# The gate table's one-hot tensors, weighed on GpSimd instead of on ScalarE and VectorE

## The reference, cut to what matters

```python
sc = einsum("thpc,hpnc->thpn", q, sub_keys)        # two halves p, 128 keys each
top_s, top_i = top_k(sc, 16)                       # per token, head and half
best_s, best_pos = top_k(cand_s, 16)               # of the 256 sums of pairs
idx  = i * 128 + j                                 # i, j: the keys of the two halves
gate = softmax(best_s)
hid  = gelu(x . u[idx]) * gate
out  = sum over the 128 picks of hid * v[idx]
```

## Time and profile before

| | us |
|---|---|
| Median of 3 runs | 2608.36 (2605.65 to 2610.68) |
| The profiled execution's own time | 2611.84 |
| Its span, first to last instruction | 2610.0 |
| TensorE busy | 2421.7 (93%) |
| VectorE busy | 1398.1 (54%) |
| ScalarE busy | 738.3 (28%) |
| GpSimd busy | 396.8 (15%) |
| Line 1053, VectorE one-hots, 96 instructions | 113.0 busy, mean 1218 ns |
| Line 1093, ScalarE weighing, 288 instructions | 89.4 busy, mean 389 ns |
| Line 757 in this phase, GpSimd fetches, 65 instructions | 103.2 busy, mean 1587 ns |

### The profile page before, as it was taken

One profiled execution on the slowest core, in us unless ns is written; L12 is line 12 of the kernel. 1 busy time (PEld: TensorE's weight loads), 2 busy tenths in 40 slices (PEclk: granted clock), 3 DMA queues, 4 the chain that ended last, 5 costly groups with the idle time before them and its releaser, 6 DMA issues. The chain is left out here.

```text
span 2610.0 us, 26901 instructions
## 1 busy us (share of the span) xinstructions
PE 2421.7 (93%) x10289; PEld 1765.2 (68%) x10289; DVE 1398.1 (54%) x2491; ACT 738.3 (28%) x1319; POOL 396.8 (15%) x305
## 2 busy tenths in 40 slices
PE   7999899799999988988989999999995999987989
PEld 4467666687555555656668888889994898875444
DVE  1235423336987967465367777766676523346021
ACT  1134412222110134435233333333333322221010
POOL 1100000000233324132121111123330000023000
PEclk9999999999999999999989999999997899986999
DMA  4220032212777767787899999977772222120210
GB/s 179 92 81 17 9 129 98 96 65 77 242 249 251 244 205 240 232 262 220 263 359 309 314 312 309 311 259 277 274 258 101 101 97 97 49 105 3 78 65 32
DMA packets 181808, 454.45 MB, mean 174 GB/s; under 512 B 15536, under 2 KB 105904, under 8 KB 174896
## 3 DMA queue, kind: packets, MB, share of 16 engines
q1 hardware_dynamic: 144816, 318.49, 36.2%
q0 software_dynamic: 36864, 134.23, 14.9%
HBM read 406.33 MB, written 46.33 MB: 173 GB/s over the span
## 5 line engine op out<-in xcount | busy, mean ns | idle before, releaser
L722 PE MATMUL bank<-XT,ur 128*128 128x384 f32 x1552 | 523.1, 494 | 30.9 <-DMA ur<-in_u 30.9
L722 PEld LDWEIGHTS bank<-XT,ur 128*128 128x128 f32 x1552 | 293.5, 193 | 234.4 <-DMA ur<-in_u 43.6
L1224 PE MATMUL bank<-Vh,Hh 128*128 128x512 f32 x768 | 300.3, 391 | 12.7 <-DVE Vl L1273 12.4
L1226 PE MATMUL bank<-Vh,Hl 128*128 128x512 f32 x768 | 300.4, 391 | 0.0
L1225 PE MATMUL bank<-Vl,Hh 128*128 128x512 f32 x768 | 300.3, 391 | 0.0
L757 POOL DMA_INDIRECT ring_c<-in_v,gidx x128 | 148.0, 1156 | 501.6 <-DVE x_res L769 390.2
L1273 DVE TENSOR_TENSOR Vl<-Vr,Vh 128x1024 fp32r<-128x1024 f32 x128 | 156.8, 1225 | 116.6 <-ACT Vh L1247 116.5
L1247 ACT ACTIVATE Vh<-Vr 128x1024 fp32r<-128x1024 f32 x128 | 135.5, 1059 | 250.3 <-PE bank L1226 222.2
L1224 PEld LDWEIGHTS bank<-Vh,Hh 128*128 128x128 f32 x768 | 144.8, 189 | 43.4 <-issue 13.0
L1053 DVE TENSOR_TENSOR hot<-tab_sb,ijg 128x1024 f32<-128x1024 f32 x96 | 113.0, 1218 | 105.5 <-PE bank L1079 98.9
L731 ACT ACTIVATE ar<-bank 128x384 f32<-128x384 f32 x97 | 47.5, 490 | 428.0 <-PE bank L722 428.0
(11 more groups left out here) (305 smaller groups left out, 4173.9 us busy)
## 6 DMA issues: line engine op xcount, KB each, us to landing
ur<-in_u SPq DMA_DIRECT2D x128, 512.0 KB, 3.5
Vr<-in_v SPq DMA_DIRECT2D x128, 512.0 KB, 5.2
W<-in_w_stream SPq DMA_DIRECT2D x27, 2048.0 KB, 7.7
gates<-stage SPq DMA_DIRECT2D x48, 512.0 KB, 6.3
Gr<-gates SPq DMA_DIRECT2D x128, 192.0 KB
early<-ar SPq DMA_DIRECT2D x97, 192.0 KB
A<-early SPq DMA_DIRECT2D x97, 192.0 KB
w_raw<-in_w_mixer SPq DMA_DIRECT2D x14, 1024.0 KB, 4.9
```

What stands on the lines that cost most here:

```text
L722: mm = pe.matmul(c.bank[bank + r][:, 0:DN], c.ur[:, r, k * P:(k + 1) * P], c.XT[:, k, 0:DN], start=k == 0, stop=k == KT - 1)
L1224: pe.matmul(ps, Hh[r][:, tok], Vh[r][:, cut], start=n == 0, stop=False)
L1226: mm = pe.matmul(ps, Hl[r][:, tok], Vh[r][:, cut], start=False, stop=n == PK - 1)
```

## The change: what it does

The one-hots are made in the other order, `hot[0]` first. GpSimd weighs all 8 tokens of `hot[0]` with one product of 128 x 1024 by a broadcast operand; ScalarE's six instructions and VectorE's one per slice are gone, with their semaphores. TensorE waits for both one-hots and for GpSimd's product. GpSimd's fetches are no longer issued ahead: each iteration waits for the first one-hot of slice j, makes the product, and then issues one fetch, or seven after the last slice of a tile.

```diff
--- before.py
+++ after.py
@@ -1029,7 +1029,6 @@
     Q = 4
     S = 2 * Q
     NSL = P // S
-    ON_ACT = 6
     EB = 4
     CUTS = 16
     PER = E_LOOP + E_GAP
@@ -1037,8 +1036,7 @@
         hot = [[ctx.enter_context(nc.sbuf_tensor(f"hot{half}{i}", [P, S, P], F32)) for i in range(2)] for half in range(2)]
         stage = ctx.enter_context(nc.sbuf_tensor("stage", [P, PK, P], F32))
         gat.buffers(ctx, "ring_b")
-        hot_made, weighed_a, weighed_d, built, copied, stored = signals(
-            nc, ctx, "hot_made weighed_a weighed_d built copied stored")
+        hot_made, weighed, built, copied, stored = signals(nc, ctx, "hot_made weighed built copied stored")
         block = ctx.enter_context(nc.Block())
         dest = t["gates"].rearrange("i j t -> j i t")
 
@@ -1049,11 +1047,8 @@
                 r, tok = j % 2, j * S
                 if j >= 2:
                     dve.wait_ge(built, 2 * (j - 1))
-                for half in (1, 0):
+                for half in (0, 1):
                     dve.tensor_tensor(hot[half][r][:], mid(c.iota, S), bc(ijg[:, half, tok:tok + S], P), ALU.is_equal).then_inc(hot_made, 1)
-                dve.wait_ge(hot_made, 2 * j + 2)
-                part = hot[0][r][:, ON_ACT:]
-                dve.tensor_tensor(part, part, bc(ijg[:, 2, tok + ON_ACT:tok + S], P), ALU.mult).then_inc(weighed_d, 1)
                 gat.dot(dve, s)
                 s += 1
                 if j % NSL == NSL - 1:
@@ -1070,8 +1065,8 @@
                 e = E_GATES + tt * PER
                 for s in range(NSL):
                     j, r = tt * NSL + s, s % 2
-                    pe.wait_ge(weighed_a, j + 1)
-                    pe.wait_ge(weighed_d, j + 1)
+                    pe.wait_ge(hot_made, 2 * j + 2)
+                    pe.wait_ge(weighed, j + 1)
                     for q in range(2):
                         if 2 * j + q >= 4:
                             pe.wait_ge(copied, 2 * j + q - 3)
@@ -1085,23 +1080,12 @@
 
         @block.scalar
         def _(act):
-            def weigh(j):
-
-                act.wait_ge(hot_made, 2 * j + 2)
-                for k in range(ON_ACT):
-                    one = hot[0][j % 2][:, k]
-                    last = act.activation(one, one, ACT.Copy, scale=ijg[:, 2, j * S + k:j * S + k + 1])
-                last.then_inc(weighed_a, 1)
-
             for tt in range(DT):
                 e = E_GATES + tt * PER
-                weigh(tt * NSL)
                 if tt >= 1:
                     act.wait_ge(stored, 16 * CUTS * tt)
                 for s in range(NSL):
                     j = tt * NSL + s
-                    if s + 1 < NSL:
-                        weigh(j + 1)
                     for q in range(2):
                         act.wait_ge(built, 2 * j + q + 1)
                         o = stage[:, :, (2 * s + q) * Q:(2 * s + q + 1) * Q]
@@ -1131,8 +1115,15 @@
 
         @block.gpsimd
         def _(pool):
-            for s in range(DOTS_CHOOSE, SLOTS):
-                gat.fetch(pool, s)
+            s = DOTS_CHOOSE
+            for j in range(DT * NSL):
+                pool.wait_ge(hot_made, 2 * j + 1)
+                one = hot[0][j % 2][:]
+                pool.tensor_tensor(one, one, bc(ijg[:, 2, j * S:(j + 1) * S], P), ALU.mult).then_inc(weighed, 1)
+                for _ in range(1 + (DOTS_GAP if j % NSL == NSL - 1 else 0)):
+                    if s < SLOTS:
+                        gat.fetch(pool, s)
+                        s += 1
```

## The result

| | us |
|---|---|
| Before, median on the same chip | 2607.01 (2601.74 to 2610.68, 4 runs) |
| Changed, median | 2842.57 (2836.19 to 2843.80, 4 runs) |
| Ratio | 1.0894, 95% interval 1.0866 to 1.0923 |
| Span of the profiled execution, before and changed | 2610.0 and 2840.9 |

The change makes the kernel 8.9% slower, some 235 us. The forecast was 2853, range 2795 to 2900.

A forecast was written before the change was run, and what follows sets the result against it. It took VectorE to bound the loops, and TensorE with its loads the stretches between. Terms 87.7 + 156.8 - 6.1 + 6.9 = +245 on 2611.84 gave 2857, less 3.5 for the median: 2853, range 2795 to 2900.

The forecast's parts named there:

- The chain: In each loop slice, one-hots, product, fetch, landing and dot run serially: 9.9 us in place of 3.87.
- The product held off by the one-hot: In each slice GpSimd's product waits for VectorE's second one-hot and ends 1.76 us after it, at 4.11.
- the rival without waiting (2812): In the loops the engines' products do not wait for each other: product ends at 3.12, slice 8.9 us; chance 0.07.
- How many slices: Lengthened loop periods: 15 in tile 0 (+87.7 us), 13 each in tiles 1 and 2 (+156.8 together).
- The slices made ahead: Two slices made ahead for each of tiles 1 and 2 stay hidden in the early-product stretch, by 10 us or more.
- The stretches: Between the loops, where early products, fetches and stores meet: 0 us taken, with 10 us either way.
- TensorE's clock: After each tile's last slice, TensorE runs slower from idling: 2.3 us three times, +6.9; bounds 0 and 6 each.
- The signs: Expected in the loops' profile: dots waiting 4 to 6 us per slice, 150 to 250 in all; product near 3.0 us.
- Landing rivals: In the loops the fetched row lands faster (2816 or 2806, chance 0.15) or slower, 4.30 us (2890, chance 0.12).
- The fast one: In the loops the row lands an estimated 3.2 us from the fetch's start: slice 8.75, time 2806; chance 0.15.
- The faster side: In the loops the row is there at the dot's turn and VectorE bounds at 3.53 us per slice: 2588; chance 0.01.
- side remark of a rival: In the loops, rows on time but GpSimd's product on the same port: 5.3 us per slice, 2660; chance 0.01.

The follow-up runs named there:

- order-only kernel: Kernel before, weighing unchanged and no GpSimd product, but each fetch waits for both one-hots of its slice; 2779.82 us, ratio 1.0655.
- kernel with the fetch ahead: Changed kernel, with GpSimd issuing the fetch of slice j before the wait and product of slice j; 2660.33 us, ratio 1.0204 to before.
- half-row kernel: Changed kernel with this phase's fetches cut to half the bytes, the dots keeping their width; 2795.42 us, ratio 1.0715.
- memset kernel: Changed kernel with fetches six slots ahead and GpSimd's product replaced by two memsets of the same tensor; 2583.96 us, ratio 0.9908.

## Why the prediction was right

**The chain.** The mechanism was found from the order of the code and its price from rows; both held. The slice was forecast with 9.89 us and is 9.81 in tile 0, 9.83 in tile 1 and 9.74 in tile 2 (147.18 / 15, 127.82 / 13, 126.62 / 13). Term by term in the slice above: product's end 4.11 (forecast 4.11); from there to the fetch's end 1.13 (1.24, since between a product and a fetch GpSimd needs 0.15 and not 0.30); landing 3.36, in the other slices of the loops 3.12 to 4.14 with a mean of 3.40 (3.40); dot 1.15 (1.14). The order-only kernel shows the chain without the product, and the kernel with the fetch ahead shows that it goes with two moved lines.

**The product held off by the one-hot.** Rows 5 were enough. The kernel that waits for both one-hots loses 7 to 10 us where overlapping work would have lost 45, so the rival without waiting (2812) is out by experiment and not by the total alone.

**How many slices.** 15 + 13 + 13 held. The slices made ahead stayed hidden, with 17.76 us to spare where I had 10 or more.

**The stretches.** I took 0 for them with 10 us either way. They gave back 4.9 and 5.4 us more than the forecast parts beside them. More than half of that is TensorE's waiting for loads of `ur`, which fell from 7.3 to 4.8 us behind tile 0 and from 7.4 to 4.1 behind tile 1, beside a DMA share of 0.94 where it was 1.00. Which transfer made room for them was not tried.

**TensorE's clock.** For the last slice of each tile and the early product behind it I took 2.3 us, and the end of tile 2 shows +5.6. The rows of TensorE at the end of tile 2, above, part it. Its products take 3.75 us in place of 2.05 and the early products 49.26 in place of 48.13 (7.53 + 41.73), together 2.8 us, at a granted clock of 0.76 from 1479.9 to 1494. That is the clock term, well inside the bounds of 0 to 6. The other 2.9 is the wait for `ur`, for which I had nothing in this place. It goes with the last six fetches, which are now issued beside that load: in the kernels that issue them there (the changed one, the order alone, the fetch ahead, the wait for both) TensorE waits 1.3 to 3.0 us for `ur` behind the last loop, with half rows 1.3, and with the fetches six slots ahead it does not wait there at all.

**The signs.** The dots' wait was named with 4 to 6 us in each slice and 150 to 250 us in all. It is 6.3 us on average in the loops and 324.9 us in all. That is a slip, not a wrong mechanism: by my own chain the dot stands from 2.35 to 8.75, so 6.4 us, 262 over 41 slices, and the dots of the stretches come on top. GpSimd's product reads 2.81 us and not 3.0, and in none of the 48 slices 1.90, since the first one-hot always releases it while VectorE is in the second. The fetch instruction reads 0.98 in the loops where I had 0.94. TensorE's wait at the first slice of tiles 1 and 2 is gone, and those products take 1.95 us. The phases behind are 3.4 us shorter.

**The total.** The forecast was +245 us, and the profiles differ by 231. The periods gave 4 us less, the two stretches 10 less, the phases behind 3 less, and the end of tile 2 gave 3 more. No large error was hidden by another one.

**Landing rivals.** The fast one (3.2 us from the fetch's start) is out: 4.34 us from start to dot. The half-row kernel gives an estimate of its split: near 2.0 us for the 512 KB and near 2.3 us for the rest, the fetch instruction's 0.98 counted in. The Trainium skill (DMA: Bandwidth & Descriptors, "Anatomy of one DMA") has 2.0 us and, by its rate, an estimate of 1.2 for the bytes. The fixed part is close to the page's, and the bytes go slower here.

**The faster side.** VectorE's own pace was put at 3.53 us and is 3.42, as the memset kernel shows, so line 1056 cost it 0.45 us per slice and not 0.34. The 5.3 us for a product taking turns with VectorE and the rows on time was a side remark of a rival with chance 0.01; measured, it is 5.12 and 2657 us, against 2660 there. It deserves its place beside the forecast: it is the loss that remains once the obvious one is mended.

## What to carry to other kernels

Before handing work to an engine that also issues transfers, write its queue down in order and ask, for each transfer, which slice will read it: a transfer that ran ahead must keep its lead, or its whole flight becomes part of the loop. Then look at what the new work reads: in these runs a GpSimd product, which reads SBUF, and a VectorE instruction with two SBUF operands ran one after the other, so moving a product from VectorE to GpSimd saved VectorE nothing (3.82 us per slice against 3.87). ScalarE took VectorE's two tokens and brought the slice to 3.52, until it was full itself. A long duration, or a wait put down to a DMA, may be a turn at SBUF: look at what ended just before.

## What the runs showed of the hardware that was not expected

- The price of holding off goes with the size of the product: GpSimd's 128 x 1024 product costs VectorE 1.70 us per slice (5.12 less 3.42), its 128 x 256 product 0.40 (3.82 less 3.42).
- GpSimd's memset of 128 x 1024 beside VectorE's two-operand dot costs neither anything that the rows show (0.96 and 1.22 us).
- A product of GpSimd that waits on VectorE is recorded from its release: 2.81 us in the changed kernel, 1.90 when released after VectorE's one-hots, 2.01 where a fetch stood ahead of it. Its end, not its length, is the number to use.
- Between a product and an indirect DMA on GpSimd there are 0.15 us, between two indirect DMAs 0.30.
- The fetch instruction on GpSimd took 0.94 to 1.00 us where VectorE stood idle and 1.67 beside VectorE's two-operand instructions.
- The landing of a gather of 128 rows, from the end of its instruction, was 3.4 us on average for 4 KB rows and 2.4 us for 2 KB rows, in loops with little other traffic (DMA share 0.26 with the full rows).
